# Delta-rule heads: GpSimd's three products moved out of the scan, VectorE's scalings and first pivots placed behind the scan's last step

## What is computed

```
k, q   = l2norm(k), l2norm(q) * 128**-0.5          # rn_k, rn_q: reciprocal roots of the sums of squares
decay  = exp(gc_i - gc_j)                          # decT, kept transposed
lower  = beta_i * (k_i . k_j) * decay, strictly lower
u, w   = solve(I + lower, [v*beta, k*beta*exp(gc)])
A      = (q_i . k_j) * decay, lower with diagonal
scan over tiles:  v_new = u - w S;  o = q S + A v_new;  S = S * g_last + k_dec^T v_new
```

## Time and profile before

| | |
|---|---|
| median of 3 runs (lowest to highest) | 2523.73 us (2523.3 to 2526.33) |
| the profiled execution | 2522.0 us |
| its span | 2520.4 us |
| PE busy | 2371.7 us (94%) |
| VectorE, ScalarE, GpSimd busy | 1371.6, 1004.3, 308.8 us |
| mean granted clock of TensorE, share of full speed | 0.978 |

### The profile page before, as it was taken

How to read it: one execution, slowest core, us unless ns; L and a number is a source line. 1 busy time by engine, 2 the same in 40 slices (tenths; PEclk the granted TensorE clock), 3 DMA queues, 4 the chain that set the end, 5 groups by cost and what they waited for, 6 DMA issues and landing times. The chain is left out here.

```text
span 2520.4 us, 49062 instructions
## 1 busy us (share of the span) xinstructions
PE 2371.7 (94%) x19072; PEld 2262.5 (90%) x19072; DVE 1371.6 (54%) x2553; ACT 1004.3 (40%) x2100; POOL 308.8 (12%) x438
## 2 busy tenths in 40 slices
PE   7888889999999999999998887999999999999998
PEld 5778779999999999999987776899999999999898
DVE  5576653677333425663556676537773344356644
ACT  4655433333234424442366554323332353255422
POOL 1222211000011101110012222100000110011000
PEclk9999899999999999999999988999999999999999
DMA  7110114111334323214221111231113332222132
GB/s 270 49 43 26 41 40 149 42 51 43 109 105 100 87 101 99 62 59 148 85 84 49 43 34 35 67 127 35 51 50 88 88 91 85 77 68 82 49 106 84
DMA packets 63262, 195.43 MB, mean 78 GB/s; under 512 B 16376, under 2 KB 16542, under 8 KB 62928
## 3 DMA queue, kind: packets, MB, share of 16 engines
q1 hardware_dynamic: 46880, 148.55, 17.8%
q0 software_dynamic: 16176, 44.07, 6.7%
HBM read 177.97 MB, written 8.39 MB: 74 GB/s over the span
## 5 line engine op out<-in xcount | busy, mean ns | idle before, releaser
L794 PE MATMUL proj<-h_hi,w_hi 128*128 128x320 f32 x3072 | 741.3, 322 | 20.8 <-issue 8.5
L794 PE MATMUL proj<-h_lo,w_hi 128*128 128x320 f32 x3072 | 706.2, 311 | 0.0
L794 PE MATMUL proj<-h_hi,w_lo 128*128 128x320 f32 x3072 | 702.0, 311 | 0.0
L2247 DVE TENSOR_TENSOR w_lo<-raw,w_hi 128x1024 fp32r<-128x1024 f32 x232 | 283.6, 1222 | 513.2 <-ACT w_hi L1623 512.1
L794 PEld LDWEIGHTS proj<-h_hi,w_hi 128*128 128x128 f32 x3072 | 510.1, 190 | 36.4 <-issue 22.9
L794 PEld LDWEIGHTS proj<-h_lo,w_hi 128*128 128x128 f32 x3072 | 519.3, 190 | 0.0
L794 PEld LDWEIGHTS proj<-h_hi,w_lo 128*128 128x128 f32 x3072 | 516.8, 189 | 0.0
L1623 ACT ACTIVATE w_hi<-raw 128x1024 fp32r<-128x1024 f32 x232 | 245.9, 1060 | 533.3 <-PE proj L794 329.7
L794 PE MATMUL mix<-area 128*128 128x128 f32 (+8 forms) x4576 | 400.1, 267 | 45.8 <-DVE area L2464 38.4
L794 PEld LDWEIGHTS mix<-area 128*128 128x128 f32 (+5 forms) x4576 | 339.4, 163 | 86.0 <-issue 59.8
L1623 ACT ACTIVATE area<-mix 128x384 f32<-128x384 f32 (+8 forms) x374 | 151.6, 426 | 583.3 <-PE mix L794 468.5
(11 more groups left out here) (319 smaller groups left out, 2677.2 us busy)
## 6 DMA issues: line engine op xcount, KB each, us to landing
raw<-in_w_in SPq DMA_DIRECT2D x128, 512.0 KB, 3.5
raw<-in_w_mb SPq DMA_DIRECT2D x96, 512.0 KB, 3.5
raw<-in_w_mod POOLq DMA_DIRECT2D x32, 512.0 KB, 4.5
area<-in_bias POOLq DMA_DIRECT2D x64, 128.0 KB, 4.7
raw<-in_w_out SPq DMA_DIRECT2D x16, 512.0 KB, 3.5
out_x<-area SPq DMA_DIRECT2D x10, 512.0 KB, 2.6
merged<-in_w_mod SPq DMA_DIRECT2D x8, 512.0 KB, 11.2
area<-area POOLq DMA_DIRECT2D x64, 64.0 KB, 1.9
```

The source lines that it names most:

```text
L794: return T.matmul(out, l, r, start=start, stop=stop)
L2247: return V.tensor_tensor(out, a_, b_, op)
```

## The change

GpSimd's first product is dropped: ScalarE makes `dec = gram[0] * beta_sq` in ten scalings of 128x128 (`A_gram_rows`), and VectorE's `A_lower` multiplies that with `decT`. `beta_sq` comes from a reciprocal on VectorE (`A_factor`), no longer from POOL's roots, and the sums of squares and the scaled beta of the values have places of their own (`sums_k`, `sums_q`; `beta_rn`, `A_values`). GpSimd's two other products (`A_masked`) run in the levels of the same head, behind VectorE's first masked copies; for the last head they run behind its `A_lower`, in the scan of head 2. On VectorE `A_scaled` and pivots 1 to 3 stand behind step 4, all other pivots and the inverse in one run ahead of `A_lo(4h+7)`, and `A_lo(4h+9)` between steps 2 and 3. On ScalarE `A_take(h+1, 1)` stands ahead of the scalings, and `A_hi(4h+9)` ahead of front unit 6.

```diff
     def A_front(h):
-        roots = stat[:, 20 * (h % 2):20 * (h % 2) + 10]
+        roots, squares = (stat[:, 20 * (h % 2) + i:20 * (h % 2) + i + 10] for i in (0, 10))
         pool.wait_ge(A_fev.sem, A_fev.at(layer, FRONT * h + 6))
         held(pool)
-        P.tensor_tensor(roots, roots, neg_half[:, 0:10], ALU.pow)
+        P.tensor_tensor(roots, stat[:, SUMS:SUMS + 10], neg_half[:, 0:10], ALU.pow)
         held(pool)
         P.drain()
-        pt(stat[:, 20 * (h % 2) + 10:20 * (h % 2) + 20], roots, roots)
+        pt(squares, roots, roots)
+        pt(beta_rn, A_head(1, h), both(rn_k(h)))
         held(pool)
         P.drain()
-        pt(beta_sq, A_head(1, h), both(rn_k_sq(h)))
-        pt(A_head(5, h), A_head(5, h), both(rn_k_sq(h)))
+        pt(A_head(5, h), A_head(5, h), both(rn_k_sq(h))).then_inc(A_rn.sem, A_rn.step)
+        if h == 0:
+            P.memset(XT, 0.0)
+        pool.wait_ge(A_own.sem, A_own.at(layer, 3 * h + 2))
+        held(pool)
+        for t in range(SP_TILES, TILES):
+            blocks_in(pool, t, A_relay_pool)
+        if h == HEADS - 1:
+            A_masked(h)
+
+    def A_masked(h):
+        decT = decTs[h % 2]
+        if h == HEADS - 1:
+            pool.wait_ge(A_lat.sem, A_lat.at(layer, h + 1))
+        else:
+            pool.wait_ge(A_x.sem, A_x.at(layer, 5 * h + 2))
+        held(pool)
+        pt(decT, decT, A_mask(tri))
         held(pool)
         P.drain()
-        pt(A_head(1, h), A_head(1, h), both(rn_k(h))).then_inc(A_rn.sem, A_rn.step)
-        if h == 0:
-            P.memset(XT, 0.0)
-        decT = decTs[h % 2]
-        pool.wait_ge(A_own.sem, A_own.at(layer, 3 * h + 1))
-        held(pool)
-        pt(dec, decT, beta_sq.unsqueeze(3).to_broadcast([128, 2, TILES, 128])).then_inc(A_dm.sem, A_dm.step)
-        pt(decT, decT, A_mask(tri))
-        pool.wait_ge(A_own.sem, A_own.at(layer, 3 * h + 2))
-        held(pool)
-        P.drain()
-        for t in range(SP_TILES, TILES):
-            blocks_in(pool, t, A_relay_pool)
         pt(decT, decT, A_both(gram[:, :, 1, :])).then_inc(A_dm.sem, A_dm.step)
...
             A_o_root(h - 1)
+        if h < HEADS - 1:
+            A_masked(h)
         if h:
...
+    def A_values(h):
+        for d in range(2):
+            for t in range(TILES):
+                A.activation(Rv[:, d, t, :], A_tmv[:, TILES + t, :], ACT.Identity, scale=beta_rn[:, d, t:t + 1])
+
+    def A_gram_rows(h, d):
+        if d == 0:
+            act.wait_ge(A_own.sem, A_own.at(layer, 3 * h + 1))
+            A.drain()
+        for t in range(TILES):
+            last = A.activation(dec[:, d, t, :], gram[:, t, 0, :], ACT.Identity, scale=beta_sq[:, d, t:t + 1])
+        if d:
+            last.then_inc(A_dm.sem, A_dm.step)
...
     A_hi(4)
     for u in (6, 7):
         A_front(0, u)
+    A_gram_rows(0, 0)
+    A_gram_rows(0, 1)
+    A_hi(5)
     A_silu_v(0)
     A_gate(0)
-    A_hi(5)
     for u in (8, 9):
         A_front(0, u)
     for h in range(HEADS):
...
             A_hi(4 * h + 7)
+            A_take(h + 1, 1)
         else:
             join_gate(0)
             A_hi(18)
         act.wait_ge(A_rn.sem, A_rn.at(layer, h + 1))
         for d in range(2):
             A_keys(h, Rk, 5, d)
-        for d in range(2):
-            A_keys(h, Rv, 1, d, TILES)
-        if more:
-            A_take(h + 1, 1)
+        A_values(h)
         act.wait_ge(A_sb.sem, A_sb.at(layer, 5 * h))
...
             A_gate(h + 1)
-            A_hi(4 * h + 9)
         for n, units in enumerate(((), (3, 4, 5), (6, 7), (8,), (9,))):
+            if more and n == 2:
+                A_hi(4 * h + 9)
+            if more and n == 3:
+                A_gram_rows(h + 1, 1)
             for u in units if more else ():
                 A_front(h + 1, u)
+            if more and n == 2:
+                A_gram_rows(h + 1, 0)
             act.wait_ge(A_va.sem, A_va.at(layer, 5 * h + n + 1))
             copy(vn, M[:, 1024:1280].rearrange("p (d c) -> p d c", d=2)).then_inc(A_vn.sem, A_vn.step)
...
     def A_decays(h):
         dve.wait_ge(A_fev.sem, A_fev.at(layer, FRONT * h + 3))
         for c, w in QUARTERS:
-            last = mul(D32[c], decTs[h % 2][c, :, :, c], lower_16[c].unsqueeze(1).unsqueeze(1).to_broadcast([32, 2, TILES, 32]))
-        last.then_inc(A_own.sem, A_own.step)
+            mul(D32[c], decTs[h % 2][c, :, :, c], lower_16[c].unsqueeze(1).unsqueeze(1).to_broadcast([32, 2, TILES, 32]))
+
+    def A_factor(h):
+        dve.wait_ge(A_fev.sem, A_fev.at(layer, FRONT * h + 6))
+        fence()
+        V.reciprocal(stat[:, INV:INV + 5], sums_k)
+        fence()
+        mul(beta_sq, ab_s[:, 40:80].rearrange("p (d h t) -> p d h t", d=2, h=HEADS)[:, :, h, :],
+            stat[:, INV:INV + 5].unsqueeze(1).to_broadcast([128, 2, TILES])).then_inc(A_own.sem, A_own.step)

     def A_blocks(h):
         dve.wait_ge(A_fev.sem, A_fev.at(layer, FRONT * h + 8))
-        dve.wait_ge(A_rn.sem, A_rn.at(layer, h + 1))
         fence()
         for c, w in QUARTERS:
             mul(D32[c], D32[c], gram[c, :, 0, c].unsqueeze(1).to_broadcast([32, 2, TILES, 32]))
...
     def A_lower(h):
         dve.wait_ge(A_dm.sem, A_dm.at(layer, 2 * h + 1))
         for d in range(2):
-            last = mul(dec[:, d], dec[:, d], gram[:, :, 0, :])
+            last = mul(dec[:, d], dec[:, d], decTs[h % 2][:, d])
         last.then_inc(A_lat.sem, A_lat.step)
...
     A_convolve(0, 2)
+    A_decays(0)
+    A_factor(0)
     A_lo(4)
-    A_decays(0)
     A_blocks(0)
     A_lower(0)
     A_lo(5)
...
         more = h < HEADS - 1
         if more:
             A_lo(4 * h + 6)
-        A_pivots(4, 9)
+        A_pivots(4, 15)
+        A_inverse(h)
         A_lo(4 * h + 7 if more else 18)
-        A_pivots(9, 15)
-        A_inverse(h)
-        if more:
-            A_convolve(h + 1, 0)
         if h:
             A_out_squares(h - 1)
         A_spread(h)
+        if more:
+            A_convolve(h + 1, 0)
         if more:
             A_convolve(h + 1, 1)
...
             split_y(h - 1, A_y, False)
-        if more:
-            A_lo(4 * h + 9)
-        else:
+        if not more:
             A_lo(19)
         dve.wait_ge(A_rest.sem, A_rest.at(layer, h + 1))
-        if more:
-            A_decays(h + 1)
         for n in range(5):
             A_step(h, n)
             if not more:
...
                 elif n == 1:
                     argument_rest()
                 continue
-            if n == 1:
+            if n == 0:
+                A_decays(h + 1)
+                A_factor(h + 1)
+            elif n == 1:
                 A_blocks(h + 1)
             elif n == 2:
                 A_lower(h + 1)
-            elif n == 3:
+                A_lo(4 * h + 9)
+            elif n == 4:
                 A_scaled(h + 1)
                 A_pivots(1, 4)
```

More of the change, by code:

```diff
@@ L113, in program @@
         gate_post = view(gate_post_t, 2, KT)
-        stat = sb("stat", [128, 64])
+        stat = sb("stat", [128, 80])
         AREA = 16800
@@ L297, in program @@
                         for d in range(2) for i in range(2))
-        BETA_SQ, O_STAT = 40, 56
+        BETA_SQ, BETA_RN, O_STAT, INV, SUMS = 40, 50, 60, 65, 70
+        beta_sq, beta_rn = (stat[:, at:at + 10].rearrange("p (d t) -> p d t", d=2) for at in (BETA_SQ, BETA_RN))
+        sums_k, sums_q = stat[:, SUMS:SUMS + 5], stat[:, SUMS + 5:SUMS + 10]
         rn_k, rn_q, rn_k_sq, rn_q_sq = (lambda h, i=i: stat[:, 20 * (h % 2) + 5 * i:20 * (h % 2) + 5 * i + 5] for i in range(4))
@@ L592, in both @@
                     return v.unsqueeze(1).to_broadcast([128, 2, TILES])
-                beta_sq = stat[:, BETA_SQ:BETA_SQ + 10].rearrange("p (d t) -> p d t", d=2)
                 def A_front(h):
-                    roots = stat[:, 20 * (h % 2):20 * (h % 2) + 10]
+                    roots, squares = (stat[:, 20 * (h % 2) + i:20 * (h % 2) + i + 10] for i in (0, 10))
                     pool.wait_ge(A_fev.sem, A_fev.at(layer, FRONT * h + 6))
                     held(pool)
-                    P.tensor_tensor(roots, roots, neg_half[:, 0:10], ALU.pow)
+                    P.tensor_tensor(roots, stat[:, SUMS:SUMS + 10], neg_half[:, 0:10], ALU.pow)
@@ L1752, in A_front @@
                         for t in range(4):
-                            last = squares(0, rn_k(h), t, t)
+                            last = squares(0, sums_k, t, t)
                     elif u == 4:
                         for t in range(4):
-                            last = squares(1, rn_q(h), t, t)
+                            last = squares(1, sums_q, t, t)
                     elif u == 5:
                         copy(A_tmv[:, 4:5, :], src(1))
-                        squares(0, rn_k(h), 4, 0)
-                        squares(1, rn_q(h), 4, 1)
+                        squares(0, sums_k, 4, 0)
+                        squares(1, sums_q, 4, 1)
                         copy(gram[:, 4, :, :], src(2, 2))
                         A.drain()
-                        A.activation(rn_k(h), rn_k(h), ACT.Copy, bias=EPS)
```

(11 more changed lines are left out.)

## The result

The change takes the kernel from 2524.46 us (median of 4 runs) to **2457.33 us** (2456.32 to 2458.89, 4 runs), a ratio of 0.9734 with a 95% interval of 0.9717 to 0.9751. Measured once more, beside the last experiments, it was 2458.47 against 2523.26 us, 0.9745 (0.9732 to 0.9759). The forecast was 2461.7 with a range of 2450 to 2488, taken from a median of 2523.73 us before; one more run of the kernel before, taken with the change, makes it 2524.46. The profiled execution has a span of 2455.1 us, 65.3 less than before.

A forecast was written before the change was run, and what follows sets the result against it. TensorE, busy 2371.7 of 2520.4 us, bounds the kernel; only its idle time and slow stretches can be won. 10.5 + 16.8 + 23.1 + 12.8 - 1.2 = 62.0 us off 2523.7 gives 2461.7 us, range 2450 to 2488.

The forecast's parts named there:

- Front of head 0: Ahead of head 0's levels, both layers: TensorE's waits of 3.59 and 3.5 us go with their half clock, 10.5 us won.
- Scans of heads 0 and 1: Both layers: step 0 starts earlier, the wait ahead of step 3 goes, step 4 follows sooner; 23.1 us won.
- Scan of head 2: Without filler ScalarE's `vn` comes 1.2 us late, yet steps 3 and 4 start earlier: 6.4 us, twice, 12.8.
- Levels: All eight: VectorE's part ends early, TensorE waits only for ScalarE with the backward half of the first product; 16.8 us won.
- GpSimd's products in the levels: Six levels: the two products lock out VectorE's next SBUF product, 0.2 us each, 1.2 lost; bounds nothing to 3.1 us.
- rival 1: VectorE's masked copies in six levels are locked out too, 1.8 us each, 11 us; time 2473; chance 0.12.
- rival 4: GpSimd starves in six levels, its memset comes late and TensorE waits: 12.3 us each, 74 us; 2534, slower; chance 0.04.
- rival 3: Slow block products have their own reason, not GpSimd; front and scans keep their waits; 2510 us; chance 0.05.
- rival 2: ScalarE is the chain in every scan, its added scalings unhidden: 15.6 us lost in six scans; 2477; chance 0.14.

The follow-up runs named there:

- experiment 4: Changed kernel with GpSimd's old product (`decT` by beta), ahead of its power chain, in place of ScalarE's ten scalings in three scans: 2458.38 us, ratio 0.9754.
- experiment 5: Changed kernel with ScalarE's copy out of `proj` (`A_take(h+1, 1)`) back behind the values' scalings, in six levels: 2457.72 us, ratio 0.9744.
- experiment 8: Changed kernel with `kd` scalings behind ScalarE's spread, SP's relay ahead of its stream and `A_scaled` behind step 3: 2439.29 us; without the `kd` move 2456.70 us.
- experiment 1: Kernel before with only GpSimd's two mask products moved into the levels, its third product staying in the scan: 2480.49 us, ratio 0.9831.
- experiment 6: Changed kernel with GpSimd's product by the mask done three times in place of once, in heads 0 to 2: 2500.02 us, ratio 0.9911.
- experiment 9: Changed kernel with `kd` scalings behind the spread, relay ahead of the stream, and GpSimd's old product in place of ScalarE's gram-row scalings: 2439.95 us.
- experiment 3: Changed kernel with ScalarE's scalings of the `gram` rows in the scan given back to GpSimd, once `gram` is there: 2473.43 us, ratio 0.9807.

## Why the prediction was right

**Front of head 0.** 10.5 us forecast, 10.5 measured. TensorE's clock in the same place as the earlier trace rows, a window of the changed kernel (length, busy time and instructions of TensorE, its weight loads, VectorE, ScalarE and GpSimd, granted clock, DMA share, GB/s):

```profile
86.00:96.00 10.00, 10.00 (x74) 9.92 (x73) 4.57 (x15) 7.09 (x18) 0.19 (x1) 1.00 0.26 73
```

Wait and half clock have both gone.

**Scans of heads 0 and 1.** The block products, `A_lower` and steps 3 to 4 (4.39 us where I worked out 4.35) came as forecast. The term was 1.5 us low in all: I gave the earlier step 0 0.74 us per scan by its two waits, and it gave 1.1.

**Scan of head 2.** 7.0 us for 6.4. The late `vn` of step 2 came as forecast, as a wait of 1.27 us for the 1.2 I gave; it costs nothing, since VectorE's update sets step 3 (experiment 4). What I left out is the same early step 0: TensorE is 2.0 us ahead at step 2. Steps 3 and 4 begin 5.1 and 7.1 us earlier, counted from the first matmul ahead of the scan, where I had 4.7 and 6.4. The wait of 1.59 us ahead of step 4 is for the most part the moved `w_lo` (1.22 us):

```profile
268.43 0.71 PE L800 MATMUL mix<-merged,area 128*128 128x128 f32 x4 [1.59 <-DVE area L2535]
```

**Levels.** The sum is right (17.6 for 15.6), the picture behind it only in part. I had TensorE do the forward half early and wait for ScalarE alone, in every stage. It waits for VectorE's spread first, 10.0 us in layer 0. The inverse leaves VectorE at 161.97, but its relay through the DMA queues takes until 166.72, 4.75 us; taking `A_lo(4h+7)` out from ahead of the inverse shortened VectorE's part and not that. In head 0 ScalarE was hardly late, by nothing in layer 0 and 0.48 us in layer 1. For the sum it did not matter, since the stage ends by its backward half; experiments 5 and 8 show that each alone. That the half clock in the levels would stay was wrong too: it became shorter in five of the eight. The waits fell by 15.5 us (from 46.0 to 30.5 in both layers, for `proj`, VectorE's and ScalarE's spread), and the other 2 I put down to clock. The sum gave each stage about 2 us and they won 1.1 to 3.5, so that the total came so close is in part luck.

**GpSimd's products in the levels.** `w_lo` took 3.14 us where I said about 3.5, the masked copies kept their time, the memset came 2.4 us early (1.9 in head 0, where I allowed 1 or less). Rivals 1 and 4 fall. The Trainium skill ("SBUF — State Buffer", section "Who interferes with whom") has an exclusive lock between VectorE and GpSimd in which the second to come blocks for the whole of the first one's instruction. Here the trace agrees in both directions: `w_lo` starts at 177.58 while GpSimd's product runs until 179.63, and ends 1.1 us after that; and GpSimd's next product, which then comes second, takes 3.70 us in place of the 2.92 of the earlier trace rows.

**Rivals.** 1, 3 and 4 are refuted by the rows above and experiments 1 and 6, rival 2 by experiments 4 and 9, for the scalings that its price was made of. Rival 4's chain itself is real: experiment 6 makes the memset late and TensorE waits for it.

## What to carry to other kernels

When a VectorE instruction takes two and a half times what its size says, look at what GpSimd does in that moment, and move the overlap, not the work: a GpSimd product beside instructions with an input in PSUM was free here, and one beside products out of SBUF cost VectorE between 1.9 us (2.99 us of GpSimd's work, experiment 3) and 3.1 us (2.92 and 3.17). When two engines feed the two halves of a step, shorten the one that comes last first; the other edit is worth nothing until then (the relay: nothing alone, about 4 us of waits behind `kd`). And ask of each item ahead of a critical one who reads it: ten scalings read only in the scan stood ahead of the spread in each of the eight levels, and cost 13.5 us in all.

## What I had not expected of the hardware

Instructions of VectorE with a single tensor input, in SBUF, are held by GpSimd's products as well. I had the casts in mind, and not the scalings of the convolutions: in experiment 6 the cast took 3.12 us in place of 0.60 and the scaling of 128x641 2.72 in place of 0.55, with GpSimd at work beside both. The Trainium skill (same page and section) says of copies, casts and `tensor_scalar` that they can take both pairs of ports, when their operands allow it, and then contend; the trace agrees.

A wait that goes takes its half clock along, and this can be a large share of what a wait costs. Mean granted clock of the kernel before, of the change, and of experiment 8 (span, clock; the die stands here for the one core that runs):

```profile
die 0 (median of its cores): 2520.4 us, clock 0.978
```

```profile
die 0 (median of its cores): 2455.1 us, clock 0.988
```

```profile
die 0 (median of its cores): 2437.7 us, clock 0.992
```

The missing 0.022 of 2520.4 are 55 us, the missing 0.012 of 2455.1 are 29: up to 26 of the 65 us may be clock (up to, because TensorE is idle in part of these stretches).
